# A fused decoder layer on one core: another order of the first feed-forward products, and eight low parts on GpSimd in place of VectorE

## The reference

```python
h = x + mix @ w_out
hn = rms_norm(h, norm_ffn_g)
return h + (jax.nn.silu(hn @ w_gate) * (hn @ w_up)) @ w_down
```

## Time and profile before

| what | value |
|---|---|
| median of 3 runs | 1287.11 us (1286.85 to 1287.22) |
| the profiled execution's own time | 1287.07 us |
| its span in the trace | 1285.3 us |
| TensorE busy | 1262.8 us, 98% of the span |
| GpSimd busy | 646.0 us, 50% |
| VectorE busy | 516.0 us, 40% |
| ScalarE busy | 378.0 us, 29% |
| mean granted clock of TensorE | 0.995 of full speed |

### The profile page before, as it was taken

The page is one execution under the profiler, slowest core; times in us unless marked ns, Lnnn a source line. Parts: engine busy times, 40 slices in busy tenths (PEclk is TensorE's granted clock), DMA queues, the critical chain, the costliest instruction groups (busy, mean ns, idle before and its releaser), DMA issues.

```text
span 1285.3 us, 21876 instructions
## 1 busy us (share of the span) xinstructions
PE 1262.8 (98%) x9082; PEld 1174.3 (91%) x9082; DVE 516.0 (40%) x942; ACT 378.0 (29%) x715; POOL 646.0 (50%) x529
## 2 busy tenths in 40 slices
PE   7999999999999999998999999999999999999997
PEld 7997788989666699998999999999999999999997
DVE  7844213433766432677323232323232323232146
ACT  6000110100677611354332323232323232323323
POOL 3453023323455341047756666666666666656735
PEclk9999999999999999998999999999999999999999
DMA  5546366252111051011112021212120212121203
GB/s 202 194 148 222 111 240 241 97 213 83 50 67 67 1 188 48 2 34 34 66 34 66 34 66 34 66 34 67 34 67 34 66 34 66 36 65 36 80 1 136
DMA packets 38098, 107.99 MB, mean 84 GB/s; under 512 B 4016, under 2 KB 16496, under 8 KB 36208
## 3 DMA queue, kind: packets, MB, share of 16 engines
q1 hardware_dynamic: 38000, 106.60, 24.1%
HBM read 95.73 MB, written 10.85 MB: 83 GB/s over the span
## 4 chain that ended last, share of the span: by engine, by line
PE 92%; DVE 3%; ACT 2%; issue 1%; POOL 1%; DMA 0%; DVEq 0%; SPq 0%; ACTq 0%
PE ps L1154 11%; PE ps L1156 11%; PE ps L1155 11%; PE ps L1188 7%; PE ps L1190 7%; PE ps L1189 6%; PE ps L719 6%; PE ps L721 6%; PE ps L720 6%; PE ps L859 3%; PE ps L904 3%; PE ps L883 2%; PE ps L928 2%; PE ps L929 2%; PE ps L930 2%; PE ps L836 1%
## 5 line engine op out<-in xcount | busy, mean ns | idle before, releaser
L1154 PE MATMUL ps<-combo,w_hi 128*128 128x264 f32 x672 | 192.7, 287 | 3.5 <-issue 3.5
L1156 PE MATMUL ps<-combo,w_lo 128*128 128x264 f32 x672 | 192.0, 286 | 0.0
L1155 PE MATMUL ps<-combo,w_hi 128*128 128x264 f32 x672 | 191.8, 285 | 0.0
L588 POOL TENSOR_TENSOR w_lo<-w_stage,w_hi 128x512 fp32r<-128x512 f32 (+1 forms) x57 | 77.5, 1361 | 183.3 <-ACT w_hi L1213 183.2
L1980 DVE TENSOR_TENSOR resid<-ps,resid 128x352 f32<-128x352 f32 x240 | 126.0, 525 | 103.5 <-PE ps L1190 103.5
L719 PE MATMUL ps<-act_hi,w_hi 128*128 128x352 f32 x480 | 158.9, 331 | 7.9 <-DVE act_lo L1642 7.9
L1188 PE MATMUL ps<-hid,w_hi 128*128 128x352 f32 x504 | 163.1, 324 | 0.7 <-DVE resid L1980 0.7
L1190 PE MATMUL ps<-hid,w_lo 128*128 128x352 f32 x504 | 162.5, 322 | 0.0
L1189 PE MATMUL ps<-hid,w_hi 128*128 128x352 f32 x504 | 162.3, 322 | 0.0
L721 PE MATMUL ps<-act_hi,w_lo 128*128 128x352 f32 x480 | 155.2, 323 | 0.0
L720 PE MATMUL ps<-act_lo,w_hi 128*128 128x352 f32 x480 | 155.0, 323 | 0.0
(11 more groups left out here) (328 smaller groups left out, 3002.0 us busy)
## 6 DMA issues: line engine op xcount, KB each, us to landing
w_stage<-in_w SPq DMA_DIRECT2D x75, 512.0 KB, 3.6
resid<-in_state_k SPq DMA_DIRECT2D x8, 1792.0 KB, 7.8
v_buf<-in_state_v SPq DMA_DIRECT2D x14, 1024.0 KB, 5.0
raw<-in_w SPq DMA_DIRECT2D x22, 512.0 KB, 3.5
resid<-in_xT SPq DMA_DIRECT2D x16, 528.0 KB, 7.7
out_yT<-resid SPq DMA_DIRECT2D x24, 176.0 KB, 1.8
q_d<-out SPq DMA_DIRECT2D x12, 176.0 KB, 4.1
out_kT<-out SPq DMA_DIRECT2D x12, 176.0 KB, 1.9
```

Of the source, the lines that this page charges most:

```text
L588: pool.tensor_tensor(w_lo_row[:, cols_], half_unit(f, product), f32(w_hi_row[:, cols_]), ALU.subtract).then_inc(half_split, 1)
L1154: pe.matmul(out, hi[:, wk], x_hi[:, k, tk], start=(k == 0 and first), stop=False, skip_group_check=not first)
L1155: pe.matmul(out, hi[:, wk], x_lo[:, k, tk], start=False, stop=False, skip_group_check=not first)
L1156: mm = pe.matmul(out, lo[:, wk], x_hi[:, k, tk], start=False, stop=(k == 3), skip_group_check=not first)
```

## The change

The change has three parts. First, TensorE's order: behind U2 it becomes (1,P7), (2,P1), (1,P4), (1,P6), (2,P2), (1,P5), (2,P7), (2,P6), (1,P3), (2,P5), (2,P4), (2,P3). A table `FIRST_POS` assigns the slots of these products, no longer their place in the order; (1,P7) now takes the slot that (1,P1) leaves, (2,P1) that of (1,P2), and (2,P2) and (1,P5) those of the up weights of tile 0. Second, the eight low parts of the second token half (A21 and A22) move from VectorE to GpSimd (`first_low`, semaphore `pool_lo`), ahead of `last_weight_sum(1)`; G2 and the first combinations of y21 wait for them. Third, the lists of GpSimd, ScalarE and VectorE are put into another order to go with the products; on VectorE `plain_hidden` now stands ahead of the low parts of S2, and the low parts of S1 ahead of the combinations of y12. Nothing that is computed changes. The diff, cut to what is spoken of:

```diff
+            def first_low(first, y, which, k):
+
+                pool.wait_ge(hi_done, first + k + 1)
+                pool.tensor_tensor(which[1][:, k, :], y[:, k, :], f32(which[0][:, k, :]), ALU.subtract).then_inc(pool_lo, 1)
+
...
             weight_sums(1)
             weight_low(1, "P1")
             weight_low(1, "P2")
+            for k in range(4):
+                first_low(8, y21, A21, k)
+            for k in range(4):
+                first_low(12, y22, A22, k)
             last_weight_sum(1)
             weight_low(1, "P7")
+            weight_low(2, "P1")
+            weight_low(1, "P4")
             weight_low(1, "P6")
-            weight_low(1, "P4")
+            weight_low(2, "P2")
             weight_low(1, "P5")
-            weight_low(2, "P1")
+            weight_sums(2)
+            weight_low(2, "P7")
+            hidden_low2(0)
+            weight_low(2, "P6")
+            hidden_low1(0)
+            last_weight_sum(2)
             weight_low(1, "P3")
-            hidden_low2(0)
-            hidden_low1(0)
-            weight_sums(2)
-            weight_low(2, "P2")
-            last_weight_sum(2)
-            weight_low(2, "P6")
             second_hidden(1)
+            weight_low(2, "P5")
             hidden_low2(1)
-            weight_low(2, "P7")
-            weight_low(2, "P5")
-            hidden_low1(1)
             weight_low(2, "P4")
             weight_low(2, "P3")
+            hidden_low1(1)
...
                         if product[0] == "G" and x == 0:
-                            pe.wait_ge(dve_lo, (k if product == "G1" else KT + k) + 1)
+                            pe.wait_ge(dve_lo if product == "G1" else pool_lo, k + 1)
...
                 combo_high(A22, y22, k, Y22_AT[k])
+            weight_high(1, "P7")
             keep_p1(1)
+            weight_high(2, "P1")
             for k in range(4):
                 combo_high(S3, s3_f, k, S3_AT[k])
             silu_second(0)
-            weight_high(1, "P7")
+            weight_high(1, "P4")
             weight_high(1, "P6")
             for k in range(4):
                 combo_high(S2, y11, k, S2_AT[k])
-            weight_high(1, "P4")
+            weight_high(2, "P2")
             weight_high(1, "P5")
-            weight_high(2, "P1")
-            weight_high(1, "P3")
             act.wait_ge(gate_done, GATE_NO[0, "U2"])
-            for k in range(4):
+            for k in range(2):
                 combo_high(S1, y21, k, S1_AT[k])
             keep_p7(1)
-            hidden_high2(0)
-            keep_u2(1)
-            hidden_high1(0)
-            act.wait_ge(dve_lo, 20)
+            for k in range(2, 4):
+                combo_high(S1, y21, k, S1_AT[k])
+            silu_first(1)
+            act.wait_ge(dve_lo, 12)
+            act.wait_ge(pool_lo, 8)
             for k in range(4):
                 combo_high(S4, y12, k, S4_AT[k])
-            weight_high(2, "P2")
-            silu_first(1)
+            weight_high(2, "P7")
+            hidden_high2(0)
+            hidden_high1(0)
+            keep_u2(1)
             weight_high(2, "P6")
+            keep_p1(2)
             silu_second(1)
-            keep_p1(2)
+            weight_high(1, "P3")
+            weight_high(2, "P5")
             hidden_high2(1)
-            weight_high(2, "P7")
-            weight_high(2, "P5")
-            hidden_high1(1)
             weight_high(2, "P4")
             weight_high(2, "P3")
+            hidden_high1(1)
...
-            combo_low(8, y21, A21, 0)
...
-            combo_low(12, y22, A22, 3)
...
+            plain_hidden()
             for k in range(4):
                 combo_low(20, y11, S2, k)
             for k in range(4):
+                combo_low(24, y21, S1, k)
+            for k in range(4):
                 combined(y12, y12, y11, k, ALU.subtract, S2_AT[k])
-            plain_hidden()
-            for k in range(4):
-                combo_low(24, y21, S1, k)
...
-FIRST_GATES = [(0, "G1"), (0, "U1"), (1, "P1"), (1, "P2"), (0, "G2"), (0, "U2"), (1, "P7"), (1, "P6"), (1, "P4"), (1, "P5"),
-               (2, "P1"), (1, "P3")] + [(2, n) for n in PRODUCTS[1:]]
+FIRST_GATES = [(0, "G1"), (0, "U1"), (1, "P1"), (1, "P2"), (0, "G2"), (0, "U2"), (1, "P7"), (2, "P1"), (1, "P4"), (1, "P6"),
+               (2, "P2"), (1, "P5"), (2, "P7"), (2, "P6"), (1, "P3"), (2, "P5"), (2, "P4"), (2, "P3")]
+FIRST_POS = {(0, "G"): 0, (0, "U"): 2, (1, "P1"): 4, (1, "P2"): 5, (1, "P7"): 10, (2, "P1"): 11, (1, "P4"): 6, (1, "P6"): 7,
+             (2, "P2"): 8, (1, "P5"): 9, (2, "P7"): 12, (2, "P6"): 13, (1, "P3"): 14, (2, "P5"): 15, (2, "P4"): 16, (2, "P3"): 17}
```

More of the change, by code:

```diff
@@ L235, in build @@
         w_split, part_split = sem("w_split"), sem("part_split")
-        half_split = sem("half_split")
+        half_split, pool_lo = sem("half_split"), sem("pool_lo")
         raw_in = [sem(f"raw_in{i}") for i in range(RAWS)]
@@ L1362, in keep_p7 @@
                 act.wait_ge(gate_done, GATE_NO[f, "P7"])
-                act.wait_ge(hidden2, f)
+                if f > 1:
+                    act.wait_ge(hidden2, f)
                 copy(b3, two_banks(0)).then_inc(p7_kept, 1)
@@ L1388, in hidden_free @@
                 elif f == 0:
-                    act.wait_ge(dve_lo, 28)
+                    act.wait_ge(dve_lo, 20)
                     act.wait_ge(y_done, 32)
                 else:
-                    act.wait_ge(dve_lo, 32)
+                    act.wait_ge(dve_lo, 24)
             def hidden_high1(f):
@@ L2009, in _ @@
             normal(y21, 1, 1, 1)
-            combo_low(8, y21, A21, 0)
             normal(y21, 2, 2, 1)
-            combo_low(8, y21, A21, 1)
             normal(y21, 3, 3, 1)
-            combo_low(8, y21, A21, 2)
             normal(y22, 0, 4, 1)
-            combo_low(8, y21, A21, 3)
             normal(y22, 1, 5, 1)
-            combo_low(12, y22, A22, 0)
             normal(y22, 2, 6, 1)
-            combo_low(12, y22, A22, 1)
             normal(y22, 3, 7, 1)
-            combo_low(12, y22, A22, 2)
-            combo_low(12, y22, A22, 3)
             first_hidden(0)
@@ L2033, in _ @@
             first_gate(1)
+            dve.wait_ge(pool_lo, 1)
             combined(y21, y21, y22, 0, ALU.add, Y22_AT[0])
+            dve.wait_ge(pool_lo, 2)
             combined(y21, y21, y22, 1, ALU.add, Y22_AT[1])
             combined(y11, y21, y11, 0, ALU.subtract, S1_AT[0])
+            dve.wait_ge(pool_lo, 3)
             combined(y21, y21, y22, 2, ALU.add, Y22_AT[2])
             combined(y11, y21, y11, 1, ALU.subtract, S1_AT[1])
+            dve.wait_ge(pool_lo, 4)
             combined(y21, y21, y22, 3, ALU.add, Y22_AT[3])
@@ L2190, in lay_out @@
             if what[1][1] == "1":
-                POS[0, what[1][0]] = pos
+                POS[0, what[1][0]] = at = FIRST_POS[0, what[1][0]]
                 SPLIT_NO[0, what[1][0]] = splits = splits + 1
-                GATE_AT[pos] = GATE_AT[pos + 1] = GATE_NO[0, what[1][0] + "2"]
+                GATE_AT[at] = GATE_AT[at + 1] = GATE_NO[0, what[1][0] + "2"]
                 pos += 2
         else:
-            POS[what], GATE_AT[pos] = pos, GATE_NO[what]
+            POS[what] = FIRST_POS.get(what, pos)
+            GATE_AT[POS[what]] = GATE_NO[what]
             SPLIT_NO[what] = splits = splits + 1
@@ L2219 @@
     "y11", "y12", "y21", "y22", "s1", "s2", "s3", "s4"))
-FIRST_LOWS = {"P7": 16, "P6": 20, "P5": 24, "P3": 28}
+FIRST_LOWS = {"P7": 8, "P6": 12, "P5": 16, "P3": 20}
 BIAS_BEHIND = [6, 7, 11, 12, 19, 20]
```

## The result

The changed kernel takes 1293.71 us (median of 5 runs, 1293.43 to 1293.99) against 1287.11 us before (5 runs, 1286.85 to 1287.35). The ratio is 1.0051, with a 95% interval of 1.0038 to 1.0064: slower by 6.6 us, forecast 5.4. The profiled execution took 1293.47 us and its span is 1291.6 us, 6.3 us more than before.

A forecast was written before the change was run, and what follows sets the result against it. TensorE, busy 98%, bounds the kernel, so only its idle time and lower clock count. (1,P5) at 604.9, the products, the 2.84 us stall and 1.62 us of clock put the down projection 5.4 us later: 1292.5 us, range 1289.0 to 1295.9.

The forecast's parts named there:

- What TensorE can give, and where: From P7's start to the first down projection, 10.92 us are lost to idle time and half clock, all the change can give.
- the three places: Kernel before: 1.80 us idle and 1.62 extra at (1,P4), 3.55 idle ahead of (1,P5), 3.03 extra for (1,P5) and (2,P1).
- The moved low parts: GpSimd's eight end by 571.1 without stalling G2; VectorE keeps 0.4 of 5.2 us, and (2,P1) stalls until 586.6.
- the lock: VectorE instructions with two SBUF inputs and GpSimd's never run in parallel; a turn of each costs 1.16 plus 0.56 us.
- The chain to (1,P5): VectorE and GpSimd work up to hidden_low2(0), then keep_u2(1), start (1,P5) at 604.9; net 1.1 us lost, bounds 603.0 and 607.
- the choice of turns: From 586.5 us VectorE and GpSimd were taken to alternate, instruction by instruction, which gives (1,P5) at 604.9.
- the row of 4.79 us: Kernel before: GpSimd's low part of P4 at 584.63 waited while VectorE went on; by this row (1,P5) starts near 607.
- rival (a): GpSimd is shut out during VectorE's 16-instruction stretch, (1,P5) starts near 607, time 1294.6 us; chance 17%.
- The pair behind the gap: (1,P5) with (2,P7) takes 8.85 us, as the pair after the long gap did before, ending at 613.75.
- The new neighbour: (1,P3) directly ahead of (2,P5) bares the chain to keep_u2(2): a 2.84 us stall, plus 1.62 us taken for the clock.
- The sum: From (1,P5) at 604.9, the first down projection comes at 632.76 in place of 627.33, 5.4 us later: 1292.5 us.
- Rival (c): VectorE and GpSimd run without exclusion in the new meetings, (1,P5) comes below 599.5, time 1280.6 us; chance 15%.

The follow-up runs named there:

- E2: The kernel before with only the eight low parts moved to GpSimd, product order and all other lists kept: 1287.51 us, ratio 1.0001.
- E5: E2 with ScalarE's four high parts of S3 ahead of the copy of P1's bank: 1287.61 us, ratio 1.0002.
- E1: The changed kernel with the eight low parts back on VectorE: 1291.78 us, ratio 1.0035.
- E4: The changed kernel with a one-column memset on VectorE behind the second low part of S2: 1291.10 us.
- E10: E9 with the copy of (2,P1)'s bank ahead of (1,P3)'s weight on ScalarE and hidden_low1(0) ahead of the third sum on GpSimd: 1285.04 us.
- E11: E10 without the one-column memset on VectorE: 1286.12 us, ratio 0.9990.
- E9: E6 with tile 0's hidden tile earlier on ScalarE and GpSimd, and keep_u2(1) right behind hidden_high2(0): 1286.91 us, ratio 0.9997.
- E3: The changed kernel with (2,P7) moved between (1,P3) and (2,P5) on all engines: 1289.13 us.
- E8: The kernel before with a one-column memset on VectorE behind the third low part of S2: 1288.92 us, ratio 1.0011.
- E6: The changed kernel with the changes of E1, E3 and E4 together: 1286.03 us, ratio 0.9991.

## Why the prediction was right, point by point

**What TensorE can give, and where.** Right. Everything lies between (1,P7) and the first down projection; 6.15 of the 6.3 us of span. One slip in the account of the kernel before: the three places add up to 10.0 us, not 10.92. Of the rest 0.49 lie in (1,P6), which took 587.68 + 0.12 - 584.40 = 3.40 us, and twice 0.16 between the stalls by start times and the idle times in brackets. The forecast doesn't use this sum.

**The moved low parts.** Right. They ended at 570.9 (forecast 571.1), G2 didn't wait, the first low part of S3 was issued at 571.10 (571.2). The last one of S3 ended at 578.2 (578.3), the last combination at 585.85 (585.9), `plain_hidden` at 586.47 (586.5), and (2,P1) started at 586.62 (586.6). That the lock is held by one engine at a time, 1.16 us and 0.56 us in turn, gave each of these to 0.2 us. That the 5.2 us of VectorE bring nothing is shown by E2 and E5; that the move costs in the new order, by E1.

**The chain to (1,P5).** The mechanism was right and the size off: 606.95 in place of 604.9, 2.05 us later, at the upper bound. The step that failed is the choice of turns over the row of 4.79 us. What I had made rival (a) came true, at its price (near 607), with 17% against 45%. E4 shows the cause by itself: with a single instruction of VectorE that reads nothing, the forecast by turns holds to 0.1 us. The pair E10 and E11 shows it a second time, 1.73 us against 7.92 for the low part.

The Trainium skill, "SBUF — State Buffer", section "Who interferes with whom", has the pair held for one whole instruction. Here a waiting GpSimd instruction was passed over by 14 that VectorE started after it; the measurement decides. That only one goes at a time, each to its end, agrees with every trace here. That the turns alternate, as the 604.9 took it, didn't hold in this stretch: there GpSimd got in only when VectorE ran an instruction that doesn't need the lock, or had none ready. It isn't a rule for all stretches either (see the last section).

**The pair behind the gap.** (1,P5) and (2,P7) took 614.46 - 606.95 = 7.51 us, forecast 8.85 by the pair after the 3.55 us: 1.34 us less at half clock, though the gap was 6.20 us. (1,P5) alone took 4.59 us here, and 4.2 to 5.4 us in the experiments that had idle time ahead of it, but 3.00 us in E9, behind 2.72 us idle. So this term of the sum was mis-sized, and why is open.

**The new neighbour.** Right. (1,P3) starts at 617.37 and would end its turn 2.91 us later, at 620.28; (2,P5) starts at 623.12, 2.84 us on, the forecast to the hundredth. The clock cost 4.53 - 2.91 = 1.62, as taken; but E1 and E4 had the same 2.68 us of idle time and then ran (2,P5) in 3.02 and 2.99 us. So the price of 1.62 was one of two cases, not a size, and that it came out is luck. E3 shows that the stall is of the order alone and goes with it.

**The sum.** 2.05 more for (1,P5), 1.34 less behind it: 633.48 in place of 632.76. The measured time lies 1.2 us above the forecast, inside the range. That the down projection is only 0.7 us off is luck too: two errors of opposite sign, the turns and the clock behind the gap, nearly cancel. Rival (c), which let the engines run side by side, is excluded by every trace: from 556 to 620 us no VectorE instruction with two SBUF inputs ran at its 0.62 us beside one of GpSimd at its 1.28.

**Not foreseen.** (2,P1) ran at half clock after its 2.16 us of idle time and took 4.53 us. It cost nothing, since (1,P5) was late by more: in E3 (2,P1) kept its clock after the same 2.16 us, took 3.00, and (2,P2) waited 1.94 us in place of 0.43.

## What to carry to other kernels

Two engines that share a lock are one engine for the instructions that take it: moving work from one to the other moved nothing off the path here while both were busy with such work, and the order of their joint list is what counts. Before a product is moved up, write down what it waits for and which products cover that wait; a bank whose copy hangs on a chain over VectorE and ScalarE wants about one product in between (2.84 us of stall without it here, none with it in E3). When a stretch is starved, a one-column instruction that doesn't take the lock, at the right place, can let the other engine in (2.6 us faster in E4, part of it the clock, and 1.1 in E10 against E11); at the wrong place it costs (1.6 us in E8).

## What the runs showed of the hardware that I had not expected

A GpSimd instruction that waits for the lock can be passed over by VectorE for as long as VectorE streams instructions with two SBUF inputs: 10.38, 10.36 and 10.36 us (the changed kernel, E1, E3), 7.92 us (E11), against 1.28 alone. Once in, it gets every second turn (1.75 us each), even against a VectorE that has its next instruction ready. A `memset` of one column lets it in (1.72 to 1.74 us, in all six kernels that had it: E4, E6 to E10). Whether that is because it reads nothing, or for another reason, wasn't varied. What else lets it in stays open: before, one that came at 577.05 in the middle of such a stream got in at the next boundary, and so did one in the profile of E5, at 585.60, 0.11 us after a boundary, as the ones that were shut out. The timeline of GpSimd in E5:

```profile
585.60 1.73 POOL L588 TENSOR_TENSOR w_lo<-raw,w_hi 128x512 fp32r<-128x512 f32 x1 [3.69 <-ACT w_hi L1222]
```

The clock after the same idle time of 2.68 us fell in one profile and stayed in two, and after 2.16 us it fell in the changed kernel and stayed in E3. A gap of 6.20 us cost 1.7 us behind it, one of 3.55 us 3.0.
